# A transformer layer with a product-key expert stage: slot weights moved to ScalarE, query low parts to VectorE, queries and top-k taken from unscaled rows

## What is computed

```python
x = x + concat([attention, pooled]) @ w_out
h = x * rsqrt(mean(x * x) + 1e-6) * norm2_g      # per token
q = (h @ wq).reshape(T, 8 heads, 2, 128)
sc = einsum('thpd,hpnd->thpn', q, subkeys)       # 128 keys for each half
v1, i1 = top_k(sc[:, :, 0], 16); v2, i2 = top_k(sc[:, :, 1], 16)
best, pos = top_k(v1[..., :, None] + v2[..., None, :], 16)
experts = i1[pos // 16] * 128 + i2[pos % 16]
gates = softmax(best)
act = gelu(einsum('tkd,td->tk', u_tab[experts], h))
x = x + einsum('tk,tkd->td', gates * act, v_tab[experts])
```

## Time and profile before

| | us |
|---|---|
| median of 3 runs (range) | 1212.05 (1209.65 to 1212.07) |
| the profiled execution | 1210.1 |
| its span | 1208.3 |
| PE busy | 1064.6 (88%) |
| POOL busy | 731.6 (61%) |
| DVE busy | 681.2 (56%) |
| ACT busy | 484.2 (40%) |
| DMA, mean over the span | 308 GB/s |

### The profile page before, as it was taken

One profiled execution on the slowest core, in us unless ns is written; L12 is line 12 of the kernel. 1 busy time (PEld: TensorE's weight loads), 2 busy tenths in 40 slices (PEclk: granted clock), 3 DMA queues, 4 the chain that ended last, 5 costly groups with the idle time before them and its releaser, 6 DMA issues.

```text
span 1208.3 us, 14991 instructions
## 1 busy us (share of the span) xinstructions
PE 1064.6 (88%) x5060; PEld 733.5 (61%) x5060; DVE 681.2 (56%) x1555; ACT 484.2 (40%) x1053; POOL 731.6 (61%) x443
## 2 busy tenths in 40 slices
PE   7999888898889877777777778999999999999998
PEld 6875444354545323322232223999999997998996
DVE  3567788879688586785675556414455554210212
ACT  5855233232312311212112114646666436554543
POOL 6834455556566544344444332986797985888885
PEclk9999898999999999999999999999999999999999
DMA  7739999999999999999999998673444554655553
GB/s 255 271 141 421 380 407 399 414 411 422 421 420 399 423 422 420 417 421 422 421 422 421 418 421 328 214 254 114 156 158 157 189 178 140 193 190 192 183 183 105
DMA packets 66099, 372.27 MB, mean 308 GB/s; under 512 B 7625, under 2 KB 8753, under 8 KB 32945
## 3 DMA queue, kind: packets, MB, share of 16 engines
q0 software_dynamic: 36864, 268.45, 53.8%
q1 hardware_dynamic: 26656, 97.02, 24.0%
q10 hardware_dynamic: 2512, 5.93, 1.5%
HBM read 369.79 MB, written 1.06 MB: 307 GB/s over the span
## 4 chain that ended last, share of the span: by engine, by line
PE 52%; DMA 26%; DVE 12%; ACT 5%; issue 3%; POOL 2%; DVEq 0%; ACTq 0%; POOLq 0%
DMA arena<-in_peer_uv,idx_all 25%; PE ps L1579 12%; PE ps L1580 12%; PE ps L1581 12%; PE ps L1876 11%; DVE arena L1344 5%; DVE wts L1354 2%; DVE arena L1486 1%; POOL arena L439 1%; PE ps L1938 1%; ACT prob L725 1%; POOL w_hl L428 1%; PE ps L1566 1%; ACT gel L718 1%; PE ps L1698 0%
## 5 line engine op out<-in xcount | busy, mean ns | idle before, releaser
L1876 PE MATMUL ps<-arena,prob 128*128 128x512 f32 x1024 | 479.7, 615 | 123.9 <-ACT prob L725 123.4
L439 POOL DMA_INDIRECT arena<-in_peer_uv,idx_all x256 | 293.0, 1145 | 349.4 <-PE ps L1876 305.9
L428 POOL TENSOR_TENSOR w_hl<-ring,w_hl 128x1024 fp32r<-128x1024 f32 x160 | 399.0, 2508 | 109.4 <-ACT w_hl L523 100.4
L1876 PEld LDWEIGHTS ps<-arena,prob 128*128 128x128 f32 x1024 | 190.2, 194 | 397.7 <-ACT prob L725 198.6
L1344 DVE CUSTOM_DVE_ANT_0 arena<-arena,xn 128x1024 f32<-128x1024 f32 x256 | 315.5, 1240 | 136.5 <-DMA arena<-in_peer_uv,idx_all 132.1
L1579 PE MATMUL ps<-xT,w_hl 128*128 128x256 f32 x760 | 217.7, 286 | 1.3 <-DVE xT L999 0.6
L1581 PE MATMUL ps<-xT,w_hl 128*128 128x256 f32 x760 | 215.0, 283 | 0.0
L1580 PE MATMUL ps<-xT,w_hl 128*128 128x256 f32 x760 | 215.0, 283 | 0.0
L523 ACT ACTIVATE w_hl<-ring 128x1024 fp32r<-128x1024 f32 x161 | 169.8, 1058 | 87.5 <-PE ps L1581 80.3
L718 ACT ACTIVATE gel<-acts 128x2 f32<-128x2 f32 (+1 forms) x130 | 26.5, 203 | 393.4 <-DVE acts L1344 393.3
L1579 PEld LDWEIGHTS ps<-xT,w_hl 128*128 128x128 f32 x760 | 145.7, 192 | 2.9 <-POOL w_hl L428 1.5
(11 more groups left out here) (302 smaller groups left out, 1172.2 us busy)
## 6 DMA issues: line engine op xcount, KB each, us to landing
ring<-in_weights SPq DMA_DIRECT2D x178, 512.0 KB, 3.5
arena<-in_peer_uv,idx_all POOLq DMA_INDIRECT x256, 12.5
arena<-in_rg_weights ACTq DMA_DIRECT2D x1, 2048.0 KB, 8.7
x<-in_x SPq DMA_DIRECT2D x2, 512.0 KB, 4.8
bias<-rel_scratch ACTq DMA_DIRECT2D x1, 1024.0 KB, 8.6
arena<-in_subkeys SPq DMA_DIRECT2D x1, 1024.0 KB, 6.8
out_x<-x ACTq DMA_DIRECT2D x4, 256.0 KB, 2.1
arena<-in_band SPq DMA_DIRECT2D x1, 768.0 KB, 6.9
```

Source lines behind the costliest of these rows:

```text
L428: pool.tensor_tensor(pair[:, 1], raw(n), pair[:, 0].bitcast(F32), ALU.subtract).then_inc(w_lo, 1)
L439: pool.indirect_dma_start(uv_slot(n), None, A["peer_uv"], bass.IndirectOffsetOnAxis(idx_all[:, h, c:c + 1], 0))\
L1876: j = pe.matmul(banks(2 + 2 * t + half), diag[:, n % GRING, :], uv_slot(n)[:, D + half * 512:D + (half + 1) * 512], start=(h == 0 and c % ...
```

## The change

Six edits, which the diff below shows at their core (declarations, the constant column block `C_N2` for `norm2_g` and the new semaphore are left out):

1. *Slot weights.* The product of gate and Gelu moves from DVE (two slots in one operation) to ACT (one operation for each slot).
2. *Low parts.* The twelve late query weights are subtracted on DVE, after certain pairs, and no longer on POOL.
3. *Unscaled queries.* The transposes take x itself; `norm2_g` is applied when the transposed rows are copied, `rinv` only in the exponential. The scaled rows are still made, for the dots, but later.
4. *First index.* Slot 0's index is the first of both searches, written at once; the gather of slot 0 waits for it alone (and for the means).
5. *Places.* Two groups of turned probabilities go to another buffer, so that their copies don't wait for the means.
6. *Order.* ACT's query copies and gate exponentials, and the top-k of head 1's first tile, trade places or go one pair later; tile 1's transposes come after slot 0, its root after pair 3, its normalisation after pair 5.

```diff
             if b == 0 and g < 4:
+                return arena[:, 512 * g:512 * g + 512]
             if b == 0:
-                return arena[:, 512 * g:512 * g + 512]
+                return prob[:, 512 * g - 2048:512 * g - 1536]
...
-                    if h < 2 and c % TOPK == 0:
+                    if h == 0 and c == 0:
+                        pool.wait_ge(first_index, 2)
+                    elif h < 2 and (c == TOPK or c == (h == 0)):
                         pool.wait_ge(half_decoded, 9 * (2 * h + c // TOPK + 1))
...
                     gather(h, c)
-                    if h == 0 and c == LATE_FROM:
-                        pool.wait_ge(w_lo, SPLIT_LATE)
-                    late = (h * SLOTS + c - LATE_FROM - 2) / SLOTS_PER_QUERY
-                    if late in range(W_X2 - SPLIT_LATE):
-                        split_lo(SPLIT_LATE + int(late))
+            pool.wait_ge(w_lo, W_X2)
...
-            mix_square(0)
+            mix_first_square(0)
+            evac_xT(1, 0, C_N2)
+            mix_second_square(0)
             pool_rows_out(1)
-            evac_xT(1, 0, None)
...
                 act.wait_ge(tk, topk_at(h, tiles[0]) + 9)
+                act.wait_ge(inv_done, norm_at(1, tiles[-1]) + 1)
...
                     act.activation(ex[:, h % 2, t, :], best[:, t, :], ACT.Exp, bias=nbest[:, t:t + 1],
-                                   accum_out=exs[:, h % 2, t:t + 1]).then_inc(ex_done, 1)
+                                   scale=rinv[:, t:t + 1], accum_out=exs[:, h % 2, t:t + 1]).then_inc(ex_done, 1)
...
-                act.wait_ge(w_done, turn)
+                h, c = divmod(n, SLOTS)
+                act.wait_ge(gates_done, gates_at(h, c // TOPK))
+                act.wait_ge(gel_done, turn)
                 for m in range(n, n + count):
+                    act.activation(wts[:, turn_cols(m, 1)], gel[:, turn_cols(m, 1)], ACT.Identity,
+                                   scale=gates[:, h % 2, m % SLOTS:m % SLOTS + 1]).then_inc(w_done, 1)
+                for m in range(n, n + count):
+                    act.wait_ge(w_done, m + 1)
...
-            evac_probT(0, range(2, 4))
-            act.wait_ge(band_mm, 2)
-            evac_probT(0, range(4, 6))
+            evac_probT(0, range(2, 6))
...
             pair_weights(0, 0)
-            load_root_table()
-            mix_square(1)
-            load_table(ACT.Gelu)
+            evac_xT(1, 1, C_N2)
             pair_weights(0, 1)
-            evac_xT(1, 1, None)
-            pair_weights(0, 2)
             for n in range(W_PQ + QUERIES_FIRST, SPLIT_LATE):
                 split_hi(n)
+            pair_weights(0, 2)
             first_queries(1)
             pair_weights(0, 3)
             turned_queries(1)
+            load_root_table()
+            mix_first_square(1)
+            mix_second_square(1)
+            load_table(ACT.Gelu)
             pair_weights(0, 4)
...
                     if h == 0 and p == 6:
+                        gate_exps(0, (1,))
+                    if h == 0 and p == 7:
                         query(QUERIES_FIRST)
                         split_hi(SPLIT_LATE + 2)
-                        gate_exps(0, (1,))
-                    if h == 0 and p == 8:
+                    if h == 0 and p == 9:
                         query(QUERIES_FIRST + 1)
-                    if h == 0 and p == 9:
+                    if h == 0 and p == 10:
                         scores_out(1)
-                    if h == 0 and p == 12:
+                    if h == 0 and p == 14:
                         gate_exps(1, (0,))
...
             mix_add(0, 1)
+            evac_xT(1, 0, C_N2)
+            for heads in (slice(0, 4), slice(4, 8)):
+                probabilities(0, 1, heads)
             dve.wait_ge(row_ld, 16)
             rstd(1, 0)
             normalised(0, with_gain=True)
-            evac_xT(1, 0, None)
-            for heads in (slice(0, 4), slice(4, 8)):
-                probabilities(0, 1, heads)
...
+                if h == 0 and t == 0:
+                    dve.tensor_copy(posf[:, 0, :, 0:1], ixu[:, 0:2, 0:1]).then_inc(first_index, 1)
+                    dve.wait_ge(first_index, 1)
+                    dve.scalar_tensor_tensor(out=idx_all[:, 0, 0:1], in0=posf[:, 0, 0, 0:1], scalar=float(NKEYS),
+                                             in1=posf[:, 0, 1, 0:1], op0=ALU.mult, op1=ALU.add).then_inc(first_index, 1)
...
-                elif h == 0 and p == 10:
+                elif h == 0 and p == 11:
                     first_eight(1, 0)
...
+            def late_query(h, p):
+
+                late, step = divmod(h * SLOTS + 2 * p - LATE_FROM + 2, SLOTS_PER_QUERY)
+                if step == 0 and 0 <= late < W_X2 - SPLIT_LATE:
+                    query_lo(SPLIT_LATE + late)
...
                     expert_dot(h, c)
                     expert_dot(h, c + 1)
-                    weights(h, c, 2, turn)
                     topk_steps(h, p)
+                    late_query(h, p)
...
+            dve.wait_ge(xn_done, xn_at(1, 0))
             expert_dot(0, 0)
             expert_dot(0, 1)
             make_gates(0, (0,))
-            weights(0, 0, 2, 1)
             mix_add(1, 0)
             expert_dot(0, 2)
             mix_add(1, 1)
             expert_dot(0, 3)
-            rstd(1, 1)
-            normalised(1, with_gain=True)
-            weights(0, 2, 2, 2)
+            evac_xT(1, 1, C_N2)
             expert_dot(0, 4)
             expert_dot(0, 5)
-            evac_xT(1, 1, None)
-            weights(0, 4, 2, 3)
...
                     expert_pair(h, p)
+                    if h == 0 and p == 5:
+                        rstd(1, 1)
+                        normalised(1, with_gain=True)
...
             head_rows(0)
-            pe.wait_ge(den_step, 3)
-            pool_mixed(1, 7)
-            keep_busy(3, 3)
...
             transposes(1, 0)
-            keep_busy(2, 3)
+            pe.wait_ge(den_step, 3)
+            pool_mixed(1, 7)
+            keep_busy(5, 3)
             first_queries(0).then_inc(q0_mm, 1)
...
             expert(0)
+            pe.wait_ge(sc0_evac, 1)
+            transposes(1, 1)
             expert(1)
-            pe.wait_ge(sc0_evac, 1)
-            keep_busy(4, 1)
-            transposes(1, 1)
             expert(2)
```

More of the change, by code:

```diff
@@ L78 @@
 F_BA, F_BL, F_UP = 82, 90, 98
[L80 removed]
+C_N1, C_PS, C_AP, C_CW, C_CB, C_BA, C_BI, C_LAM, C_MP, C_QG, C_N2, C_END = 0, 8, 12, 20, 52, 60, 68, 76, 84, 92, 94, 102
 def bc(ap, axis, n):
@@ L229, in prob_group @@
         def prob_group(b, g):
+            if b == 0 and g < 4:
+                return arena[:, 512 * g:512 * g + 512]
             if b == 0:
-                return arena[:, 512 * g:512 * g + 512]
+                return prob[:, 512 * g - 2048:512 * g - 1536]
             if g < 4:
@@ L650, in _, with mix_first_square @@
             load_root_table()
-            def mix_square(t):
+            def mix_first_square(t):
                 act.wait_ge(mix_added, 2 * t + 1)
@@ L658, in mix_square, with mix_second_square @@
                                scale=1.0 / D).then_inc(half_sq, 1)
+            def mix_second_square(t):
                 act.wait_ge(mix_added, 2 * t + 2)
@@ L1245, in topk_stage @@
                         dve.match_replace(cand2[:, t, :], best[:, t, 0:8], cand[:, t, :], FLT_LOW)
-                    i = dve.tensor_scalar(nbest[:, ts], best[:, ts, 0], -1.0, None, ALU.mult)
+                    dve.wait_ge(inv_done, norm_at(1, tiles[-1]) + 1)
+                    i = dve.scalar_tensor_tensor(out=nbest[:, ts], in0=best[:, ts, 0], scalar=-1.0, in1=rinv[:, ts],
+                                                 op0=ALU.mult, op1=ALU.mult)
                 elif stage == 8:
@@ L1286, in first_eight @@
                 step(8, dve.tensor_reduce(dec[:, t, :, top], eq[:, pair, top, 0:half], AX, ALU.add))
-                step(9, decode(h, 5, (t,), top))
+                step(9, decode(h, 5, (t,), slice(1, half) if h == 0 and t == 0 else top))
             def next_eight(h, t, steps):
@@ L1307, in make_gates @@
                 dve.wait_ge(gt_step, n)
+                if h >= 2:
+                    dve.wait_ge(w_done, (h - 1) * SLOTS)
                 dve.tensor_tensor(gates[:, h % 2, :].rearrange("p (t k) -> p t k", t=NT)[:, ts], ex[:, h % 2, ts],
@@ L1319, in topk_steps @@
                         query_lo(W_PQ + QUERIES_FIRST + 1)
-                elif h == 0 and p == 10:
+                elif h == 0 and p == 11:
                     first_eight(1, 0)
-                elif h == 0 and 11 <= p < 15:
-                    next_eight(1, 0, NEXT_STEPS[p - 11])
+                elif h == 0 and 12 <= p < 16:
+                    next_eight(1, 0, NEXT_STEPS[p - 12])
                 elif h == 1 and p == 0:
@@ L1347, in expert_dot @@
                     topk_stage(h + 1, c)
-            def weights(h, c, count, turn):
-                n = h * SLOTS + c
-                dve.wait_ge(gates_done, gates_at(h, c // TOPK))
-                dve.wait_ge(gel_done, turn)
```

(14 more changed lines are left out.)

7 lines of the change are left out of this document (4 added, 3 removed).

## The result

| | before | after |
|---|---|---|
| median of 6 runs | 1210.82 us (1209.65 to 1212.07) | 1203.77 us (1203.60 to 1204.93) |
| profiled execution, span | 1210.1, 1208.3 | 1203.6, 1201.6 |
| busy: DVE, ACT, POOL | 681.2, 484.2, 731.6 | 653.0, 534.1, 695.6 |

After against before is 0.9937, with a 95% interval of 0.9926 to 0.9948. That is 7.05 us less by the medians; 7.8 was forecast. The kernel before was run again beside the changed one, and over all six of its runs its median is 1.2 us lower than the one I forecast on.

The account below looks back on a forecast made before the run. The prediction took the stream of expert-row gathers at 421 GB/s to bound the kernel. Earlier start 2.8, shortage at 140 us 3.0 and shortage from 200 to 390 us 2.0 sum to 7.8 us, so 1204.3; range 1200 to 1210.

Parts of the forecast that it names:

- The bound: From 86 to 735 us the gather stream sets the time: start, bytes at 421 GB/s, and 8.0 us of shortage.
- Term 1: Start of the stream: earlier queries and values of tile 1 let gather 1 issue at 81.5, not 84.33; 2.8 us gained.
- five filler products ... at 1.46/6 = 0.24 each: On PE before the first queries: filler takes 1.2 us and ends last, so queries start at about 69.4.
- Worth nothing beyond gather 1's time: Gather 0 at the start, issued near 77.6 on the first index alone: no gain beyond that of gather 1.
- Term 2: Shortage at 140 to 156 us: the new order on ACT frees gather 22 earlier; 3.0 of 3.9 us back.
- Term 3: Shortage from 200 to 390 us: POOL no longer splits query weights, DVE subtracts instead; 2.0 of 4.1 us back.
- At nothing: Parts given no time, chiefly slot weights on ACT: 252 operations of at most 0.20, at most 51 us, covered.
- That only the start counts: Slots 8 to 13 stay late and the stream still runs short; gain 2.8 us, 1209.2; chance 0.25.
- That all shortage goes: Both shortages, at 140 and 200 to 390 us, vanish wholly; gain 10.8 us, 1201.2; chance 0.12.
- The slower one: Twelve late copies, slots 19 to 107, burden DVE at 1.23 us each; 1224, or 1217 half hidden; chance 0.05.
- The blocked gather: Each late copy on DVE holds a gather's issue by its whole 1.23 us; 14.8 us, 1219; chance 0.03.
- New stretches under 400 GB/s: A sign that the prediction is wrong: such stretches of the stream appear beside DVE's copies.

Follow-up runs that it names:

- index_with_all: The changed kernel with gather 0 waiting for all eight indices of slot 0 again; 1205.67 us, ratio 0.9949.
- query_first: The changed kernel with ACT's old order (query copies before gate exponentials, a pair earlier) and head 1's first top-k as before; 1208.58 us, ratio 0.9976.
- order_alone: The kernel before with only the new order of query copies, gate exponentials and head 1's first top-k; 1207.00 us, ratio 0.9967.
- low_on_pool: The changed kernel with the twelve late low parts subtracted on POOL between gathers again; 1204.24 us, ratio 0.9946.
- low_parts_twice: The changed kernel with each of the twelve late low parts subtracted twice on DVE; 1204.39 us, ratio 0.9944.
- softplus_spread: The changed kernel with DVE's 26 small softplus operations of head 4 spread over pairs 8 to 15, four each; 1204.18 us, ratio 0.9942.

## Why the prediction was right, and where its steps were not

The time forecast, 1204.3, was 0.5 us from the median, by steps of which some were off and made up for each other. By bytes, the start brought 1.6 us (2.1 from the head rows) for 2.8, the stop at 140 us 3.8 for 3.0, and the lead grew by 4.0 more up to 400 us for 2.0. Then 1.0 was lost at 480 to 520 us and 1.4 at the end, for which the sum had no term. The places and the mechanisms were right; that the sum came so close is in part luck.

**The bound.** "Its end is where it starts plus its bytes at 421 GB/s plus the time in which it runs short" held up to 400 us. It fails at the end, where the stream does not stop at 421 GB/s but thins out to one engine: of the 9.4 us by which the bytes were ahead at 400 us, 7.0 came out, and 1.4 of the loss is that the last 7.22 us moved 86 GB/s for 170. The step takes the run-out as the same in both kernels, and it was not.

**Term 1, 2.8 us: mechanism right, size too large.** Gather 1 moved by 2.10 against the head rows, and by 1.58 in the two profiles, whose head rows ended 0.5 apart. The mis-sized step is "five filler products ... at 1.46/6 = 0.24 each". The x6 of the earlier trace rows counts records, and a product leaves two: the five took 2.16 us for 1.2. Queries began at 70.83 for 69.4, values at 78.50 for 77.5. Against the head rows the values began 2.37 us earlier, for 2.85, and took 3.46 for 3.70. As large a miss is the step from the values to gather 1, which the prediction left at 0.28: it is 0.79, in the runs with later values too, so the values still release it, and what the 0.5 us are stays open. "Worth nothing beyond gather 1's time", on gather 0, held in the sum (1.6 us of bytes for the 1.58 of gather 1), but edit 4 is not free of value: index_with_all, without it, is 1.9 us of bytes behind, nearly all that the start gave. The first index and the earlier values are needed together.

**Term 2, 3.0 us: right, and larger than said.** Gather 22 was forecast at 135.3 and came at 136.12, before 141.10; the rate was forecast over 400 and is 420. As a part by itself it was undersized: query_first says 4.8 us by the medians, order_alone 4.6. In query_first the stop takes 3.6 us of bytes at 140 to 156 and 2.0 in the stretch behind it, which the prediction did not count. The timeline says that the query copy carries it, with a wait of 4.65 us for PE ahead of the exponentials and their two table loads (3.1 us). No run moves the copy alone, so its share is argued.

**Term 3, 2.0 us: right in place, half of what came back in bytes.** 412 became 421 GB/s, all of the 4.1 us and not half, and DVE went from 156.72 to 140.01 busy. "It loses in stalls" was right, that the stalls were the product's was not: low_on_pool moves them onto the dots. Both edits together bring about 2.4 us of time, either undone alone 0.5 to 1.8, within the intervals.

The Trainium skill, SBUF — State Buffer, section Who interferes with whom, says that DVE with two SBUF inputs contends with a GpSimd instruction that reads SBUF. The trace agrees: the dot, with two inputs from SBUF, has a mean of 1415 ns beside POOL's splits and 1224 without. The prediction left open whether the rule holds for a gather's issue. The traces show that the issue is lengthened beside DVE's work: in the kernel after it takes 0.94 us in all 64 cases without a dot or other two-input work on DVE beside it. It takes 1.49 on the mean and up to 1.98 in the 65 cases in which a dot is already running when it begins. The dot, at 1224 ns, is not lengthened. With the copies doubled POOL is busy 7.5 us longer from 200 to 390 us (94.20 for 86.71), and the time is the same within the interval.

**At nothing.** The slot weights on ACT cost more than their bound, which was no bound: 287 ns each by the page against 0.20, 60.8 us in all and not 51.

```profile
L729 ACT ACTIVATE wts<-gel,gates 128x1 f32<-128x1 f32 x252 | 60.8, 287 | 12.0 <-ACT gel L722 0.4
```

From the Gelu's start to the diagonals is 131.21 - 130.53 = 0.68 us, where the prediction had 0.47 to 0.5. ACT's share went from 40% to 44%, and no stretch shows a price; the cover named (the distance of the pairs) held.

**The rivals.** That only the start counts: refuted by 420 GB/s at 140 us. That all shortage goes: the rates say yes for both stretches, the time says no, for the 2.4 us lost at 480 to 520 us and at the end. The slower one, DVE burdened by the late copies: refuted by low_parts_twice, which doubles them without a price. The blocked gather: the issues are longer beside DVE's work, up to twice, and the time does not follow, as the prediction said. "New stretches under 400 GB/s": one, 490 to 510 us at 392, not beside the copies but behind the softplus; what it costs is not settled by softplus_spread.

## What to carry to other kernels

Look first for the wait that stands in front of unrelated work on an in-order engine: a copy that waited 5 us for PE held a Gelu, the Gelu held a freed slot, and the new order brought 4.6 us by itself, where all six edits bring 7. Count the bytes of a long DMA stream, and look at its last few us apart: here 1.4 us of the lead was lost there, and low_on_pool, with more shortage in the middle, lost less there. A stall by contention belongs to the pair of engines and not to the instruction on which it is seen, so taking that instruction away moves it (the dots went from 1224 to 1415 ns); take away the other side.

## What the runs showed that was not expected

- The stream of 256 gathers ends on one of sixteen DMA engines: the DMA share is 0.05 over the last 3.2 us in both kernels. What the last 7.22 us move differs from run to run of the experiments, from 86 to 200 GB/s.
- A small ACTIVATE on one column with a scale from SBUF takes 287 ns, where the Gelu on two columns takes 204.
- A filler product (f32, 128x256) leaves two records of 0.216 us, so the count behind a PE row is not a count of products.
- The issue of a gather takes 0.94 us alone and up to 1.98 when a dot is already running on DVE.
- The end of the head rows varied by up to 1.2 us between profiled executions of kernels that are the same up to there, while the distance from there to gather 1 agreed to 0.02 us in eight kernels. Positions are best compared from the last common instruction.
